# Expert stage of a decoder layer: GpSimd's index copies and carrier arithmetic replaced by ScalarE copies and semaphore increments

## The chip, the core and the metric

The kernel is one program on one core of a Trainium2 chip. The metric is the device time of one execution in microseconds, the median over the runs. TensorE, VectorE (DVE), ScalarE (ACT), GpSimd (POOL) and SyncE (SP) each run their own instruction stream and meet at semaphores. "PE" is TensorE and "DMA" stands for the 16 engines that move data between HBM and the core's memory.

## What is computed

One layer of a decoder: a mixing sub-layer, which the change does not touch, then a layer of 16384 single-neuron experts over 1024 tokens of width 1024. In the reference, cut to what matters:

```python
def peer(h, w_query, sub_keys, expert_u, expert_v):
    ...
    idx = jnp.take_along_axis(cand_i, best_pos, axis=-1)   # 8 heads x 16 experts for each token
    gates = jax.nn.softmax(best_s, axis=-1)
    ...
        u = jnp.take(expert_u, idx_blk, axis=0)
        act = jax.nn.gelu(jnp.einsum('thkd,td->thk', u, h_blk))
        vv = jnp.take(expert_v, idx_blk, axis=0)
        return jnp.einsum('thk,thkd->td', g_blk * act, vv)
```

So each token takes 128 experts; for each of them a row of `expert_u` (1024 floats, 4 KB) is dotted with the token, the result goes through gelu and a gate, and a row of `expert_v` is added with that weight.

## The kernel before, in words

The first 1.43 ms hold the mixing sub-layer, the search for the experts and the making of a dense table of gates. Then comes `experts` (line 1764), in which the change lies, and a short `finish` (line 2188).

`experts` splits the 1024 tokens in two. The first 640 (`DENSE`) are done densely: every expert is computed for every token on TensorE, and a table of gates, mostly zeros, picks what counts. The last 384 tokens, three tiles of 128 (`GATHERED`), fetch their own rows. Both kinds of work are cut into the same 64 steps (`NSTEP`), and a step has 256 experts of the dense kind and, for each of the three gathered tiles, two of the 128 experts that each of its tokens takes, so six row numbers for each partition.

A step c of the dense kind is, in four engines' queues:
- SP loads `un`, rows of expert_u (1 MB; half of it in every fourth step, where an earlier stage has done the other half ahead and only its result `ex_pre` is loaded), `vn`, rows of expert_v (1 MB) and the gate block `w` (640 KB).
- TensorE turns `un` (`turn`, line 1944), multiplies it with the tokens (`hide`, line 1952, 24 matmuls of 320 columns a unit) and multiplies the weighed result with `v` (`share`, line 1959, 10 units of 6 matmuls of 512 columns). In TensorE's step j it hides step j+1, then shares step j with the turns of step j+2 between the shares. Steps have 4 units of hide and turn, but every fourth (`units`) has 2.
- ScalarE splits values into a high part (`h_hi`, `ex_v_hi`, `ex_c_hi`) and does the gelus.
- VectorE makes the low parts (`split_u` line 2093, `split_v` line 2098, line 2137), multiplies by the gates (line 2132) and adds six of the ten share units from PSUM into `acc` (line 2150). `split_v(c+1)` comes once all shares of step c are done; then `weigh` of step c+2, then the adds of step c+1. TensorE has four PSUM banks for what it hands over, and reuses one when the work on it is done (`freed`).

The gathered kind lies between these on VectorE: in each step six dot products of a gathered `u` row with the token (`row_dot`, line 2103, a 128x1024 multiply with reduction) and six multiply-adds of a gathered `v` row (`row_add`, line 2116). Three are in `weigh`, three in `add`. There are three buffers for u rows and three for v rows, so each buffer is used twice a step. VectorE's instruction increments `row_used` when it has done with a buffer.

GpSimd does nothing in this stage but refill those buffers, twelve times a step in a fixed order (`rows`, line 1911). Each `refill` waits for its count of `row_used`, then does a tiny multiply of one column (`carry_wait`, line 1897: the wait is on that instruction, and the gather behind it in the queue has none), and then issues the gather (line 1893), an indirect DMA of 128 rows of 4 KB (512 KB) whose row numbers stand in a tile `ex_row`. For the first refill of a step, `indices` (line 1901) first copies the step's 12 row numbers from `g_row` into one of two `ex_row` tiles at a fixed address, and a `drain` of GpSimd stands between that copy and the gather:

```python
            def refill(c, s, slot, all_rows, to, col, done, n=2 * ROWS):
                pool.wait_ge(row_used, c * SLOTS + slot)
                carry_wait(slot - 1)
                if slot == 1:
                    indices(c, s, n)
                gather(all_rows, to[col % 3], s, col, done[col % 3])
```

Of the kernel before, what the change touches and what calls it, by code (L numbers as in the profile page):

```python
# [22 lines left out]
U32 = mybir.dt.uint32  # L23
ALU = mybir.AluOpType
ACT = mybir.ActivationFunctionType
AX = mybir.AxisListType

P = 128
# [18 lines left out]
GATHERED = 3  # L47
# [1716 lines left out]
def experts(nc, core, t, expert_u, expert_v, h, h_rows, acc, g_row, g_gate, ahead):  # L1764
# [11 lines left out]
    PERIOD = 4  # L1776
    PER = 4 * PERIOD - 2
    ROWS = 2 * GATHERED
    SLOTS = 2 * ROWS
# [7 lines left out]
    u_row = [core.at(f"ex_u_row{k}", 140 + 4 * k, [P, D]) for k in range(3)]  # L1787
    v_row = [core.at(f"ex_v_row{k}", 152 + 4 * k, [P, D]) for k in range(3)]
    row = [core.at(f"ex_row{s}", 94 + s / 16, [P, 2 * ROWS], U32) for s in range(3)]
    dot, act_dot, coef = (core.at(f"ex_{n}", 94.25 + k / 16, [P, ROWS]) for k, n in enumerate(("dot", "act_dot", "coef")))  # L1790
    carry = core.at("ex_carry", 94.5, [P, SLOTS])
    u_rows = expert_u[0].rearrange("(i j) d -> j i d", j=NKEYS)
    v_rows = expert_v[0].rearrange("(i j) d -> j i d", j=NKEYS)
    gates = g_gate[:].rearrange("p n g -> p (n g)")
# [1 line left out]
    u_row_in, v_row_in = core.sems("ex_u_row_in", 3), core.sems("ex_v_row_in", 3)  # L1796
    turned, u_hi, u_lo, v_hi, v_lo, hidden, gelued, weighed, c_hi, c_lo, summed, added = (
        core.sem(f"ex_{n}") for n in ("turned", "u_hi", "u_lo", "v_hi", "v_lo", "hidden", "gelued", "weighed", "c_hi", "c_lo",
                                      "summed", "added"))
    row_used, dotted, dot_gelued, pre_in, cleared = (  # L1800
        core.sem(f"ex_{n}") for n in ("row_used", "dotted", "dot_gelued", "pre_in", "cleared"))

    def units(j):

        return 2 if j % PERIOD == PERIOD - 1 else 4

    def before(i, j, n):


        return i * PER + (j // PERIOD * PER + 4 * (j % PERIOD) + n)  # L1810
# [6 lines left out]
    def ut(hh, e, k, n=1):  # L1817
        at = slice(DENSE + e * P, DENSE + (e + 1) * P)
        return hh[:, k, at] if n == 1 else hh[:, k:k + n, at]
# [20 lines left out]
    NI = NSTEP // PERIOD - 1  # L1840
# [21 lines left out]
    with nc.Block() as block:  # L1862

        @block.sync
        def _(sp):
            load_w(sp, 0, 0)
            load_u(sp, 0, 0)
            load_w(sp, 1, 1)
            load_u(sp, 0, 1)
            load_v(sp, 0)  # L1870
            for half in range(2):
                sp.wait_ge(ahead.stored[half], ahead.BLOCKS * 16)

            def step(i, j, c):
                load_w(sp, c + 2, j % 2)
                load_u(sp, i, j + 2)
                if j == 1:
                    load_pre(sp, i)
                load_v(sp, c + 1)

            with sp.Fori(0, NI) as i:
                for j in range(PERIOD):
                    step(i, j, i * PERIOD + j)
            for j in range(PERIOD - 2):
                step(NI, j, NI * PERIOD + j)
            load_v(sp, NSTEP - 1)

        @block.gpsimd
        def _(pool):
            u_all, v_all = expert_u[0], expert_v[0]  # L1890

            def gather(all_rows, to, s, col, done):
                nc.gpsimd.indirect_dma_start(to[:], None, all_rows, bass.IndirectOffsetOnAxis(row[s][:, col:col + 1], 0)).then_inc(done, 16)  # L1893

            def carry_wait(n):

                nc.gpsimd.tensor_tensor(carry[:, n:n + 1], g_gate[:, 0, 0:1], g_gate[:, 0, 0:1], ALU.mult)  # L1897

            def indices(c, s, n):

                nc.gpsimd.tensor_copy(row[s][:, 0:n], g_rows[:, bass.ds(c * ROWS, n)])
                pool.drain()

            def refill(c, s, slot, all_rows, to, col, done, n=2 * ROWS):

                pool.wait_ge(row_used, c * SLOTS + slot)
                carry_wait(slot - 1)
                if slot == 1:
                    indices(c, s, n)
                gather(all_rows, to[col % 3], s, col, done[col % 3])  # L1910

            def rows(c, s, last=False):
                for k in range(3):
                    refill(c, s, 2 * k + 1, u_all, u_row, 3 + k, u_row_in, ROWS if last else 2 * ROWS)
                    refill(c, s, 2 * k + 2, v_all, v_row, k, v_row_in)
                for k in range(3):
                    if not last:
                        refill(c, s, 2 * k + 7, u_all, u_row, ROWS + k, u_row_in)
                    refill(c, s, 2 * k + 8, v_all, v_row, 3 + k, v_row_in)

            g_rows = g_row[:].rearrange("p n g -> p (n g)")
            nc.gpsimd.tensor_copy(row[2][:, 0:ROWS], g_rows[:, 0:ROWS])
            pool.drain()
            for k in range(3):
                gather(u_all, u_row[k], 2, k, u_row_in[k])
            with pool.Fori(0, NSTEP // 2 - 1) as i:
                for s in range(2):
                    rows(i * 2 + s, s)
            rows(NSTEP - 2, 0)
            rows(NSTEP - 1, 1, last=True)  # L1930

        @block.tensor
# [88 lines left out]
        @block.scalar  # L2021
        def _(act):
            act.sem_inc(u_hi, PRIME)
            act.sem_inc(v_hi, PRIME)
            act.sem_inc(gelued, PRIME)
            act.sem_inc(c_hi, PRIME)

            def split_u(i, j, banks):
                for q in range(units(j)):
                    act.wait_ge(turned, before(i, j, q + 1 + PRIME))  # L2030
                    nc.scalar.activation(ut(h.hi, q // 2, (q % 2) * 4, 4), core.bank[banks[q]].rearrange("p (k n) -> p k n", k=4),  # L2031
                                         ACT.Copy).then_inc(u_hi, 1)

            def split_v(c):
                act.wait_ge(vn_in, c * 16 + 16)
                act.wait_ge(summed, c * NU + PRIME)
                nc.scalar.activation(vh.hi[:], vn[:], ACT.Copy).then_inc(v_hi, 1)  # L2037

            def gelu(i, j, banks):
                c, s = i * PERIOD + j, j % 2  # L2040
                for n in range(4):
                    e, half = n // 2, n % 2
                    x = act_out[n % 2][:] if n < units(j) else pre[:, half, :]
                    if n < units(j):
                        act.wait_ge(hidden, before(i, j, n + 1 + PRIME))
                        act.wait_ge(c_lo, c * 4 + (n - 1 + PRIME))
                        nc.scalar.activation(x, core.bank[banks[n]][:, 0:HD], ACT.Gelu_apprx_tanh).then_inc(gelued, 1)
                    act.wait_ge(weighed, c * 4 + (n + 1 + PRIME))
                    if n == 0:
                        act.wait_ge(summed, c * NU + (PRIME - NU))  # L2050
                    nc.scalar.activation(ch[s].hi[:, e, half * HD:(half + 1) * HD], x, ACT.Copy).then_inc(c_hi, 1)  # L2051

            def gelu_dots(c, part):
                act.wait_ge(dotted, c * 2 + (part + 1))
                to = slice(3 * part, 3 * part + 3)
                nc.scalar.activation(act_dot[:, to], dot[:, to], ACT.Gelu_apprx_tanh).then_inc(dot_gelued, 1)

            def step(i, j, turning=True):
                c = i * PERIOD + j
                gelu_dots(c, 0)  # L2060
                if turning:
                    split_u(i, j + 2, TURN_BANKS[j])
                if j < PERIOD - 1 or turning:
                    split_v(c + 1)
                gelu_dots(c, 1)
                if turning:
                    gelu(i, j + 2, HIDE_BANKS[(j + 1) % PERIOD])

            split_u(0, 0, range(4))
            gelu(0, 0, range(4))  # L2070
            split_u(0, 1, range(4))
            split_v(0)
            gelu(0, 1, HIDE_BANKS[0])
            with act.Fori(0, NI) as i:
                for j in range(PERIOD):
                    step(i, j)
            for j in range(PERIOD):
                step(NI, j, j < PERIOD - 2)

        @block.vector  # L2080
        def _(dve):
# [188 lines left out]
def decoder_layer(nc, x, c, w_mod, b_mod, norm1_g, w_in, b_forget, ln_v_g, w_spatial, b_spatial, w_branch_a, w_branch_b,  # L2270
          w_out, norm2_g, w_query, sub_keys, expert_u, expert_v, final_g, out):
    with ExitStack() as ctx:
        core = Core(nc, ctx)
# [47 lines left out]
        ahead.place("sc", 184, 192)  # L2321
        t.WB = 64
        t.w_dram = core.dram("w_dram", [NKEYS // 2, P, DENSE // t.WB, 2 * t.WB])
        g_row, g_gate = core.at("g_row", 200, [P, P, GATHERED], U32), core.at("g_gate", 201.5, [P, P, GATHERED])
        scatter(nc, core, t, pick_i, pick_j, gate, g_row, g_gate, ahead)
        core.end_second()
        acc = core.at("acc", 0, [P, TT, D])
        experts(nc, core, t, expert_u, expert_v, h2, h_rows, acc, g_row, g_gate, ahead)
        finish(nc, core, t, final_g, acc, out)

# [20 lines left out]
```

## Time and profile before

| | |
|---|---|
| median of 3 runs | 3462.18 us (3461.8 to 3464.92) |
| the profiled execution: its time, its span | 3472.52 us, 3470.8 us |
| `experts`, from the first gather to the last row add | 1432 to 3431 us of the span |
| busy over the span: PE, DVE, ACT, POOL | 3104.2 us (89%), 2614.3 us (75%), 1083.0 us (31%), 1471.4 us (42%) |
| granted TensorE clock, mean of the span | 0.953 |
| DMA moved | 760.68 MB, mean 219 GB/s |

How to read it: the busy share is an average over stages; `experts` is 58% of the span, and there all of TensorE, VectorE and the DMA engines are busy most of the time, so what counts is who waits for whom in a step. A timeline row gives start, duration, engine, line, operation, and in brackets how long the engine was idle before it and what ended the idle time; "issue" is time in which the engine waited for nothing that the profile shows.

### The profile page before, as it was taken

To read this page: it belongs to the slowest core of one execution; us is meant where nothing else is said; L and a number is where in the kernel's file an instruction comes from. 1 tells how busy PE (TensorE), PEld (TensorE's weight loads), DVE (VectorE), ACT (ScalarE), POOL (GpSimd) and SP (SyncE) were. 2 spreads that over 40 slices of the span, in tenths; PEclk is the share of its full clock that TensorE was granted. 3 is DMA by queue.
4 is the path that set the end of the run, shared out by engine and by line. 5 is a ranking of instruction groups with operands and counts; after the bars stand their busy time and mean duration, and the time that the engine had idled before them with its cause. 6 is when DMAs were issued, how large, how long until landed. Compare 5 with 4: busy or idle time off the path is not lost. (4 is left out here: it accounts for less than half of the span.)

```text
span 3470.8 us, 53965 instructions
## 1 busy us (share of the span) xinstructions
PE 3104.2 (89%) x18277; PEld 2734.5 (79%) x18277; DVE 2614.3 (75%) x5246; ACT 1083.0 (31%) x1837; POOL 1471.4 (42%) x1715
## 2 busy tenths in 40 slices
PE   7999999998967788899999999989999999999992
PEld 4998888787756678788788888878887888788881
DVE  5464343553899999488888888888888888888887
ACT  3223666223343366322222222222222222222221
POOL 0001000010355100066666666666666666666664
PEclk9999999998988899999999999999999999999996
DMA  6344432333000168688777887778877778777776
GB/s 245 126 152 147 121 107 77 113 127 113 25 25 0 47 203 268 226 289 304 283 283 297 304 296 293 283 278 302 294 297 286 283 291 311 285 288 293 283 285 236
DMA packets 331852, 760.68 MB, mean 219 GB/s; under 512 B 20348, under 2 KB 171480, under 8 KB 331744
## 3 DMA queue, kind: packets, MB, share of 16 engines
q0 software_dynamic: 115712, 419.48, 32.8%
q1 hardware_dynamic: 214976, 335.65, 28.3%
q10 hardware_dynamic: 1056, 4.19, 0.3%
q8 instruction: 57, 0.93, 0.1%
q14 instruction: 51, 0.42, 0.0%
HBM read 686.86 MB, written 72.39 MB: 219 GB/s over the span
## 5 line engine op out<-in xcount | busy, mean ns | idle before, releaser
L1893 POOL DMA_INDIRECT ex_u_row<-in_expert_u,ex_row x384 | 439.3, 1144 | 450.7 <-issue 431.7
L2116 DVE SCALAR_TENSOR_TENSOR acc<-ex_v_row,ex_coef,acc 128x1024 f32<-128x1024 f32 x384 | 492.4, 1283 | 108.2 <-DMA ex_v_row<-in_expert_v,ex_row 83.7
L1959 PE MATMUL psum<-ex_v_hi,ex_c_lo 128*128 128x512 f32 x1280 | 440.7, 426 | 129.8 <-issue 51.4
L2103 DVE CUSTOM_DVE_ANT_0 ex_u_row<-ex_u_row,h_rows 128x1024 f32<-128x1024 f32 x384 | 469.0, 1221 | 106.9 <-DMA ex_u_row<-in_expert_u,ex_row 106.2
L1893 POOL DMA_INDIRECT ex_v_row<-in_expert_v,ex_row x384 | 458.6, 1194 | 57.0 <-issue 32.4
L1897 POOL TENSOR_TENSOR ex_carry<-g_gate 128x1 f32<-128x1 f32 x765 | 359.1, 469 | 217.9 <-DVE ex_dot L2103 108.8
L1959 PE MATMUL psum<-ex_v_lo,ex_c_hi 128*128 128x512 f32 x1280 | 413.3, 405 | 0.0
L1959 PE MATMUL psum<-ex_v_hi,ex_c_hi 128*128 128x512 f32 x1280 | 408.9, 402 | 0.0
L1959 PEld LDWEIGHTS psum<-ex_v_hi,ex_c_lo 128*128 128x128 f32 x1280 | 226.7, 197 | 177.7 <-issue 102.9
L1952 PE MATMUL psum<-h_hi,h_lo 128*128 128x320 f32 x1792 | 303.6, 312 | 6.9 <-DVE h_lo L2093 4.5
L1952 PE MATMUL psum<-h_lo,h_hi 128*128 128x320 f32 x1792 | 300.6, 310 | 0.0
L1952 PE MATMUL psum<-h_hi 128*128 128x320 f32 x1792 | 299.2, 309 | 0.0
L1959 PEld LDWEIGHTS psum<-ex_v_lo,ex_c_hi 128*128 128x128 f32 x1280 | 250.4, 196 | 59.2
L1959 PEld LDWEIGHTS psum<-ex_v_hi,ex_c_hi 128*128 128x128 f32 x1280 | 249.1, 195 | 58.6
L1952 PEld LDWEIGHTS psum<-h_hi,h_lo 128*128 128x128 f32 x1792 | 274.7, 189 | 19.5 <-issue 11.9
L2150 DVE TENSOR_TENSOR acc<-psum,acc 128x512 f32<-128x512 f32 x384 | 263.3, 686 | 17.0 <-issue 13.1
L1952 PEld LDWEIGHTS psum<-h_lo,h_hi 128*128 128x128 f32 x1792 | 273.7, 189 | 0.0
L1952 PEld LDWEIGHTS psum<-h_hi 128*128 128x128 f32 x1792 | 272.0, 188 | 0.0
L2051 ACT ACTIVATE ex_c_hi<-ex_g 128x320 fp32r<-128x320 f32 x224 | 105.8, 472 | 505.4 <-DVE ex_g L2132 505.4
L2031 ACT ACTIVATE h_hi<-psum 128x512 fp32r<-128x512 f32 x224 | 130.9, 593 | 325.6 <-PE psum L1944 229.3
L2037 ACT ACTIVATE ex_v_hi<-ex_vn 128x2048 fp32r<-128x2048 f32 x64 | 122.8, 1919 | 339.3 <-PE psum L1959 299.9
L2098 DVE TENSOR_TENSOR ex_v_lo<-ex_vn,ex_v_hi 128x2048 fp32r<-128x2048 f32 x64 | 148.8, 2324 | 10.9 <-issue 9.8
(303 smaller groups left out, 5444.6 us busy)
## 6 DMA issues: line engine op xcount, KB each, us to landing
ex_vn<-in_expert_v SPq DMA_DIRECT2D x64, 1024.0 KB
ex_un<-in_expert_u SPq DMA_DIRECT2D x48, 1024.0 KB
w_dram<-sc_w SPq DMA_DIRECT2D x10, 4096.0 KB, 13.5
ex_w<-w_dram SPq DMA_DIRECT2D x64, 640.0 KB
gm_wm<-in_w_mod SPq DMA_DIRECT2D x16, 1024.0 KB, 5.1
pj_raw<-in_w_in SPq DMA_DIRECT2D x11, 1024.0 KB, 7.7
qk_dram<-pj_staged_r POOLq DMA_DIRECT2D x32, 256.0 KB, 3.2
gt_raw<-in_w_in SPq DMA_DIRECT2D x16, 512.0 KB, 3.9
```

The source lines that it names most:

```text
L1893: nc.gpsimd.indirect_dma_start(to[:], None, all_rows, bass.IndirectOffsetOnAxis(row[s][:, col:col + 1], 0)).then_inc(done, 16)
L1897: nc.gpsimd.tensor_tensor(carry[:, n:n + 1], g_gate[:, 0, 0:1], g_gate[:, 0, 0:1], ALU.mult)
L1952: last = nc.tensor.matmul(core.bank[bank][:, 0:HD], lhsT, rhs, start=m == 0, stop=m == len(ops) - 1)
L1959: last = nc.tensor.matmul(out, lhsT, rhs, start=m == 0 and not kept, stop=m == len(ops) - 1, skip_group_check=kept)
L2031: nc.scalar.activation(ut(h.hi, q // 2, (q % 2) * 4, 4), core.bank[banks[q]].rearrange("p (k n) -> p k n", k=4), ACT.Copy).then_inc(u_hi, 1)
L2037: nc.scalar.activation(vh.hi[:], vn[:], ACT.Copy).then_inc(v_hi, 1)
L2051: nc.scalar.activation(ch[s].hi[:, e, half * HD:(half + 1) * HD], x, ACT.Copy).then_inc(c_hi, 1)
L2098: nc.vector.tensor_tensor(vh.lo[:], vn[:], vh.hi[:].bitcast(F32), ALU.subtract).then_inc(v_lo, 1)
L2103: nc.vector.tensor_tensor_reduce(out=u_row[k % 3][:], in0=u_row[k % 3][:], in1=h_rows[:, k % 3, :], scale=1.0, scalar=0.0, op0=ALU.mult, o ...
L2116: nc.vector.scalar_tensor_tensor(out=to, in0=v_row[k % 3][:], scalar=coef[:, k:k + 1], in1=to, op0=ALU.mult, op1=ALU.add).then_inc(row_use ...
L2150: nc.vector.tensor_tensor(to, core.bank[SHARE_BANKS[j][n] if turning else LAST_SHARE_BANKS[j][n]], to, ALU.add).then_inc(added, 1)
```

## The change

The tiny multiply before each gather becomes an increment of a semaphore that nobody waits on (`carried`), issued by GpSimd behind the same wait. The copy of the row numbers and the drain leave GpSimd. ScalarE makes that copy in each step for the step after, behind its second small gelu (`gelu_dots(c, 1)`), and GpSimd's first refill of a step waits for ScalarE's count (`indexed`). `g_row` is kept as float32, as ScalarE reads it, and the copy converts to uint32. Step 0's numbers are copied before the stage's first split.

```diff
-    carry = core.at("ex_carry", 94.5, [P, SLOTS])
...
-            def carry_wait(n):
-
-                nc.gpsimd.tensor_tensor(carry[:, n:n + 1], g_gate[:, 0, 0:1], g_gate[:, 0, 0:1], ALU.mult)
-
-            def indices(c, s, n):
-
-                nc.gpsimd.tensor_copy(row[s][:, 0:n], g_rows[:, bass.ds(c * ROWS, n)])
-                pool.drain()
-
-            def refill(c, s, slot, all_rows, to, col, done, n=2 * ROWS):
+            def refill(c, s, slot, all_rows, to, col, done):
 
                 pool.wait_ge(row_used, c * SLOTS + slot)
-                carry_wait(slot - 1)
                 if slot == 1:
-                    indices(c, s, n)
+                    pool.wait_ge(indexed, c + 2)
+                pool.sem_inc(carried, 1)
                 gather(all_rows, to[col % 3], s, col, done[col % 3])
...
-            g_rows = g_row[:].rearrange("p n g -> p (n g)")
-            nc.gpsimd.tensor_copy(row[2][:, 0:ROWS], g_rows[:, 0:ROWS])
-            pool.drain()
+            pool.wait_ge(indexed, 1)
+            pool.sem_inc(carried, 1)
...
+            def indices(c, s, n=2 * ROWS):
+
+                nc.scalar.activation(row[s][:, 0:n], g_rows[:, bass.ds(c * ROWS, n)], ACT.Copy).then_inc(indexed, 1)
+
+            def step(i, j, turning=True, final=False):
                 c = i * PERIOD + j
                 gelu_dots(c, 0)
...
                 gelu_dots(c, 1)
+                if not final:
+                    indices(c + 1, (j + 1) % 2, 2 * ROWS if turning or j < PERIOD - 2 else ROWS)
                 if turning:
                     gelu(i, j + 2, HIDE_BANKS[(j + 1) % PERIOD])
 
+            indices(0, 2)
+            indices(0, 0)
...
-        g_row, g_gate = core.at("g_row", 200, [P, P, GATHERED], U32), core.at("g_gate", 201.5, [P, P, GATHERED])
+        g_row, g_gate = core.at("g_row", 200, [P, P, GATHERED]), core.at("g_gate", 201.5, [P, P, GATHERED])
```

## Rows read from the trace of the kernel before

**Rows 1.** Busy by stretch, expert stage: us, PE, PEld, DVE, ACT, POOL, clock, DMA share, GB/s

```profile
1480.00:3400.00 1920.00, 1790.02 (x9828) 1583.65 (x9826) 1634.02 (x2405) 461.35 (x871) 1244.66 (x1565) 0.97 0.79 291
```

**Rows 2.** Waits of VectorE, 1480 to 3440: waiter, releaser, us in total, times, longest

```profile
DVE ex_u_row L2103 <- DMA ex_u_row<-in_expert_u,ex_row: 106.2, 85, 3.5
DVE acc L2116 <- DMA ex_v_row<-in_expert_v,ex_row: 83.7, 55, 3.8
```

**Rows 3.** Timeline of GpSimd: the stage's first step, then a step in its middle

```profile
1471.99 0.19 POOL L1901 COPY ex_row<-g_row 128x12 uint32 x1
1473.23 1.00 POOL L1893 DMA_INDIRECT ex_u_row<-in_expert_u,ex_row  x1 [1.05 <-issue]
...
2422.61 0.45 POOL L1901 COPY ex_row<-g_row 128x12 uint32 x1
2429.34 1.53 POOL L1893 DMA_INDIRECT ex_u_row<-in_expert_u,ex_row  x1 [6.28 <-issue]
...
2432.68 0.98 POOL L1893 DMA_INDIRECT ex_u_row<-in_expert_u,ex_row  x1 [0.15 <-issue]
```

**Rows 4.** Waits of GpSimd, 1500 to 3420

```profile
POOL ex_u_row L1893 <- issue: 429.0, 248, 8.5
```

**Rows 5.** By source line, whole span: duration ns min/median/max, first and last start

```profile
L1897 POOL TENSOR_TENSOR ex_carry<-g_gate x765: 194/212/1647, 1471.7 to 3425.9; 128x1 f32<-128x1 f32 x192
L1893 POOL DMA_INDIRECT ex_u_row<-in_expert_u,ex_row x384: 944/978/3037, 1431.9 to 3415.6; - x192
```

**Rows 6.** Busy by short stretches, columns as in rows 1

```profile
2427.00:2430.00 3.00, 3.00 (x20) 2.65 (x19) 2.79 (x5) 0.44 (x1) 0.66 (x1) 1.00 0.06 26
2444.00:2448.00 4.00, 3.90 (x26) 3.45 (x24) 3.79 (x6) 2.13 (x2) 2.21 (x5) 1.00 1.03 421
```

**Rows 7.** Timeline of TensorE: the first hide matmuls of eight of its steps

```profile
1495.38 1.33 PE L1952 MATMUL psum<-h_hi,h_lo 128*128 128x320 f32 x8
...
1524.06 1.33 PE L1952 MATMUL psum<-h_hi,h_lo 128*128 128x320 f32 x8
...
2444.83 1.43 PE L1952 MATMUL psum<-h_hi,h_lo 128*128 128x320 f32 x8
...
2474.61 1.33 PE L1952 MATMUL psum<-h_hi,h_lo 128*128 128x320 f32 x8
...
2503.30 1.35 PE L1952 MATMUL psum<-h_hi,h_lo 128*128 128x320 f32 x8
...
2536.83 1.33 PE L1952 MATMUL psum<-h_hi,h_lo 128*128 128x320 f32 x8
...
2567.67 1.44 PE L1952 MATMUL psum<-h_hi,h_lo 128*128 128x320 f32 x8
...
3336.62 1.41 PE L1952 MATMUL psum<-h_hi,h_lo 128*128 128x320 f32 x8
```

**Rows 8.** Timeline of VectorE: three v splits, one first add, one dot

```profile
1498.33 2.29 DVE L2098 TENSOR_TENSOR ex_v_lo<-ex_vn,ex_v_hi 128x2048 fp32r<-128x2048 f32 x1 [0.17 <-issue]
...
1528.10 2.29 DVE L2098 TENSOR_TENSOR ex_v_lo<-ex_vn,ex_v_hi 128x2048 fp32r<-128x2048 f32 x1 [0.17 <-issue]
...
1541.77 0.68 DVE L2150 TENSOR_TENSOR acc<-psum,acc 128x512 f32<-128x512 f32 x1
...
2434.26 1.23 DVE L2103 CUSTOM_DVE_ANT_0 ex_u_row<-ex_u_row,h_rows 128x1024 f32<-128x1024 f32 x1 [1.61 <-DMA ex_u_row<-in_expert_u,ex_row]
...
2511.84 2.29 DVE L2098 TENSOR_TENSOR ex_v_lo<-ex_vn,ex_v_hi 128x2048 fp32r<-128x2048 f32 x1 [0.16 <-issue]
```

**Rows 9.** Timeline of TensorE: the end of its long wait in the step of 2503

```profile
2526.24 1.22 PE L1959 MATMUL psum<-ex_v_hi,ex_c_lo 128*128 128x512 f32 x2 [3.60 <-issue]
```

**Rows 10.** By source line, ScalarE's small gelu of the dots: duration ns min/median/max

```profile
L2056 ACT ACTIVATE ex_act_dot<-ex_dot x128: 183/188/209, 1481.3 to 3423.9; 128x3 f32<-128x3 f32 x128
```

**Rows 11.** Waits of VectorE in the stage's tail, 3368 to 3435

```profile
DVE ex_u_row L2103 <- DMA ex_u_row<-in_expert_u,ex_row: 8.0, 3, 3.5
DVE acc L2116 <- DMA ex_v_row<-in_expert_v,ex_row: 4.2, 4, 1.3
```

More of the change, by code:

```diff
@@ L1799, in experts @@
                                       "summed", "added"))
-    row_used, dotted, dot_gelued, pre_in, cleared = (
-        core.sem(f"ex_{n}") for n in ("row_used", "dotted", "dot_gelued", "pre_in", "cleared"))
+    row_used, dotted, dot_gelued, pre_in, cleared, indexed, carried = (
+        core.sem(f"ex_{n}") for n in ("row_used", "dotted", "dot_gelued", "pre_in", "cleared", "indexed", "carried"))
+    g_rows = g_row[:].rearrange("p n g -> p (n g)")
     def units(j):
@@ L1913, in rows @@
                 for k in range(3):
-                    refill(c, s, 2 * k + 1, u_all, u_row, 3 + k, u_row_in, ROWS if last else 2 * ROWS)
+                    refill(c, s, 2 * k + 1, u_all, u_row, 3 + k, u_row_in)
                     refill(c, s, 2 * k + 2, v_all, v_row, k, v_row_in)
@@ L2056, in gelu_dots @@
                 nc.scalar.activation(act_dot[:, to], dot[:, to], ACT.Gelu_apprx_tanh).then_inc(dot_gelued, 1)
-            def step(i, j, turning=True):
+            def indices(c, s, n=2 * ROWS):
+                nc.scalar.activation(row[s][:, 0:n], g_rows[:, bass.ds(c * ROWS, n)], ACT.Copy).then_inc(indexed, 1)
+            def step(i, j, turning=True, final=False):
                 c = i * PERIOD + j
@@ L2077, in _ @@
             for j in range(PERIOD):
-                step(NI, j, j < PERIOD - 2)
+                step(NI, j, j < PERIOD - 2, j == PERIOD - 1)
         @block.vector
```

## The prediction

> **What bounds the kernel now.** I first read the busy time of the expert stage by stretches [rows 1]: of 1920 us TensorE is busy 93%, VectorE 85%, the DMA engines 79% at 291 GB/s, GpSimd 65%, ScalarE 24%. No engine is full, so the next view is who waits. VectorE waits 106.2 us for gathered u rows and 83.7 us for gathered v rows [rows 2], though each buffer has half a step between two uses. So the gathers are issued late, and the timeline of GpSimd says why [rows 3]: behind the copy of the row numbers the next gather starts 6.28 us later, with GpSimd waiting for nothing that the profile shows. Only the drain stands between the two. In the stage's first step, where the only gathers so far had been issued 40 us before [rows 5], the same gap is 1.05 us. Such gaps add up to 429.0 us, the longest 8.5 [rows 4]; other gathers have 0.15 us before them [rows 3], so with 248 - 64 = 184 of those at 0.15, 401 us lie behind the 64 copies, 6.3 us each. While it lasts the DMA engines run empty: share 0.06 and 26 GB/s from 2427 to 2430, against 421 GB/s from 2444 to 2448 [rows 6]. I read this as a drain that holds GpSimd until its gathers in flight have landed. The cost reaches VectorE as a late row (the dot at 2434.26 waited for one [rows 8]), and TensorE through VectorE.
>
> How much reaches the end is read from TensorE's steps [rows 7]. Sixty steps, fifteen periods of four, run from 1495.38 to 3336.62: 122.75 us a period, 30.69 a step. One period, begun at 2444.83, has steps of 29.78 (A), 28.69 (B), 33.53 (C) and 30.84 us (D). C is the step with 2 units of hide instead of 4, so it ought to be TensorE's shortest; in it TensorE waits for VectorE, at last 3.60 us [rows 9]. Call S the start of TensorE's hides and T the start of VectorE's split_v. In C T-S was 2511.84 - 2503.30 = 8.54 us; in a step where VectorE is on time it is 1498.33 - 1495.38 = 2.95 [rows 7, 8]. From T to the end of the first add, which gives TensorE its bank back, is 1541.77 + 0.68 - 1528.10 = 14.35 us of VectorE's own work [rows 8]. In the step of 2503 this gives 2511.84 + 14.35 = 2526.19, and TensorE resumes at 2526.24 [rows 9]. From there to the next S are 10.6 us (2536.83 - 2526.2). So C = (T-S) + 14.35 + 10.6: TensorE's short step is set by VectorE.
>
> **The change part by part.**
> *The drain goes.* Rows then never have to make up 6.3 us of lost issuing. A gather takes 2434.26 - 2429.34 = 4.9 us from issue to use with the queue empty [rows 3, 8]. Twelve row operations on six buffers bring a buffer round every 14.6 us, so some 13 us are left for it. I take VectorE's waits inside the periods as gone. Then T-S in C falls to 2.95 and C becomes 2.95 + 14.35 + 10.6 = 27.9; another C, begun at 1524.06, has T-S of 4.04, which shows that the term varies with lateness, and I take 28.1. D has the units of A and should fall to A's 29.78; I take 29.9 for some time at the lower clock after C's wait. A and B already run at TensorE's pace and stay. Sum: 29.78 + 28.69 + 28.1 + 29.9 = 116.5 us, 6.3 less than 122.75; times 15 is 94 us.
> *The tail.* The last steps have few or no hides, so VectorE sets the end, and it waits 8.0 + 4.2 us for rows [rows 11]. The last rows depend on the last dots, so I count 9 of these 12.
> *The carriers.* 765 multiplies of 0.21 us median, up to 1.65, leave GpSimd [rows 5] and increments come in. GpSimd is not the bound once the drain is gone: 1244.66 us busy in 62.6 steps is 19.9 us of a 29 us step. Counted at nothing; the cover is those 9 us of GpSimd. If the increment cost nothing the gathers start up to 0.4 us earlier, which only adds to the 13 us. No row shows an increment on GpSimd in this stage; below, nothing; above, what the drain costs (a rival).
> *The copy on ScalarE.* 65 instructions of about 0.19 us, the price of a small activation [rows 10]. They stand behind the second small gelu and ahead of the gelus of the hides. ScalarE is busy 24% [rows 1]. Counted at nothing. Without cover it would cost 65 x 0.19 = 12 us.
> *The new wait.* GpSimd's first refill of step c+1 waits for a copy that ScalarE makes right after its split of v, while the refill needs the first dot of the next weigh, behind VectorE's 2.29 us split of v [rows 8]. The copy is there about 3 us before. Queued behind the wait are only gathers.
> *DMA.* The same bytes: 291 GB/s x 30.69 us = 8.9 MB a step, at 29.1 us a step 307 GB/s, below the 421 seen. SP's loads are not moved. Without the drain they share the engines with gathers at all times.
> The DMA page of the Trainium skill ("DMA: Bandwidth & Descriptors", Specifications) gives about 358 GB/s as HBM's limit for a core. The row of 421 GB/s over 4 us speaks against that as a ceiling here; with it the mean demand would still fit, and only in VectorE's weigh (six gathers and vn, 4.2 MB in 11.5 us) would some 0.2 us a step be missing, an estimate of 13 us less gain.
>
> **Sum.** 94 + 9 = 103 us. The profiled execution took 3472.5, so 3369.5; it stands 10.3 us above the median of the runs shown, so the median is forecast at 3359 us.
>
> **Rivals.**
> *Rows stay late in part.* The gathers, now always queued, and SP's loads press on each other, or a gather under load takes over 13 us. For: the engines are full (share 1.03) in bursts [rows 6]. Against: a mean share of 0.79 x 30.69 / 29.1 = 0.83. If half of the 190 us of waits stay, half of the gain stays: 3462 - 52 = 3410 us. The same page (Queues, rings and completion order) says that each DMA engine takes the queue rows in turn, packet by packet, which would halve SP's rate beside a full gather queue; no number here hangs on it.
> *A larger gain.* If the wait in C also becomes too short for the clock to fall behind it, and VectorE itself runs freer without GpSimd's arithmetic: the mean clock of 0.97 [rows 1] is worth 3% of 122.75 = 3.7 us a period, of which I put 1.5 behind this wait (its first two matmuls take 1.22 us [rows 9]), so 15 x 1.5 us, and up to 15 us more: 3359 - 38 = 3321 us.
> The SBUF page of the Trainium skill ("SBUF — State Buffer", Summary) says that a VectorE instruction with two SBUF inputs and a GpSimd one that reads SBUF block each other, the second waiting the first out. The 1647 ns carriers agree; for VectorE it would mean up to five carriers of 0.2 us in each C, 15 us, which no row shows.
> *No change.* The gap is not the drain but something each step's first gather pays. For: it is always at that gather. Against: 1.05 us in the first step. Time: 3460 us.
> *Slower.* A semaphore increment on GpSimd waits, as the drain does, for the gathers in flight. Place: before each of the twelve gathers of a step. It decides from the point where one gather with its increment takes over 29.1 / 12 = 2.4 us. With the 6.3 us of the drain and 0.98 of the gather it is 7.3 x 12 = 87 us a step, so 87 - 30.7 = 56 us more a step, and the kernel would take 3462 + 64 x 56 = 7050 us. Against: the increment is not meant to order anything; for: only that no row shows one.
>
> **How the numbers follow.** Forecast 73%, rows late in part 14%, larger gain 5%, no change 4%, slower 4%. Range: the forecast's own unknowns are C at 27.9 to 28.6 and D at 29.8 to 30.8 (+-15 us), ScalarE's 12 us and the tail's 9; it reaches down to most of the larger gain, 3325, and up to the partial case, 3415. A measurement of this kernel can tell 0.2%, 7 us, from no change. Faster by more than that 92%, within 4%, slower 4%.
>
> **What would show it.** Right: no gap over 2 us between gathers where VectorE had freed the buffer; VectorE's waits for rows under 30 us in total; T-S in C about 3 us; C about 28 and a period about 116.5; no stretch of 3 us with DMA under 0.1. TensorE still waits some 4 us in each C for the first add. Wrong in size: T-S in C stays above 4, or A and B lengthen (loads of SP late, seen as ScalarE's split of v or TensorE's turns waiting). Wrong in kind: gaps of 5 us before each step's first gather, or before every gather.

## The result, and the profile after

The changed kernel takes 3365.06 us (median of 4 runs, 3361.81 to 3366.06), beside 3463.55 us for the kernel before on the same chip: a ratio of 0.9713, 95% interval 0.9697 to 0.973, or 98.5 us less. Forecast were 3359 us in a range of 3325 to 3415. The saving in us differs between chips, through the kernel before: on another chip that takes 3452.27 us and the changed kernel 3364.79 (e6 below), so 87.5 us less.

Busy time by stretch over the expert stage, with the columns of [rows 1] (us, PE, PEld, DVE, ACT, POOL, clock, DMA share, GB/s):

```profile
1480.00:3300.00 1820.00, 1755.78 (x9833) 1573.24 (x9833) 1646.14 (x2412) 472.37 (x931) 975.76 (x752) 0.98 0.87 308
```

TensorE is now busy 96% of the stage (93% before), VectorE 90% (85%), and the DMA engines move 308 GB/s instead of 291. Then the waits of GpSimd from 1480 to 3340, and those of VectorE, which answer to [rows 4] and [rows 2]:

```profile
POOL ex_u_row L1893 <- DVE ex_dot L2101: 421.3, 240, 3.4
POOL ex_v_row L1893 <- DVE acc L2114: 327.5, 189, 3.2
POOL ex_v_row L1893 <- issue: 58.5, 192, 0.3
POOL ex_u_row L1893 <- issue: 44.3, 138, 2.5
```

```profile
DVE acc L2114 <- DMA ex_v_row<-in_expert_v,ex_row: 3.6, 2, 2.9
```

GpSimd now stands idle because VectorE has not yet freed a buffer, which is how it should be; the unexplained gaps of up to 8.5 us are gone (the longest is 2.5 us, once, at the stage's end). VectorE's waits for rows fell from 189.9 us to under 4. The timeline of GpSimd around a step's first gather, to hold against [rows 3]:

```profile
2423.62 0.94 POOL L1893 DMA_INDIRECT ex_u_row<-in_expert_u,ex_row  x1 [1.17 <-DVE ex_dot L2101]
2425.72 2.46 POOL L1893 DMA_INDIRECT ex_v_row<-in_expert_v,ex_row  x1 [1.16 <-DVE acc L2114]
2429.79 1.76 POOL L1893 DMA_INDIRECT ex_u_row<-in_expert_u,ex_row  x1 [1.62 <-DVE ex_dot L2101]
2431.86 1.24 POOL L1893 DMA_INDIRECT ex_v_row<-in_expert_v,ex_row  x1 [0.30 <-issue]
```

The gather at 2429.79 is the first of its step: 1.62 us before it instead of 6.28, and they are a wait for the dot that frees its buffer. The increments show as 0.30 us ahead of a gather that waits for nothing else.

The steps of TensorE (first hide matmuls) and VectorE (split of v, first add of C), which answer to [rows 7, 8, 9]; S and T are as in the prediction:

```profile
1492.66 1.33 PE L1942 MATMUL psum<-h_hi,h_lo 128*128 128x320 f32 x8
...
1521.35 1.33 PE L1942 MATMUL psum<-h_hi,h_lo 128*128 128x320 f32 x8
...
1538.64 0.72 PE L1949 MATMUL psum<-ex_v_hi,ex_c_lo 128*128 128x512 f32 x2 [3.65 <-DVE acc L2148]
...
1549.51 1.33 PE L1942 MATMUL psum<-h_hi,h_lo 128*128 128x320 f32 x8
...
1579.18 1.33 PE L1942 MATMUL psum<-h_hi,h_lo 128*128 128x320 f32 x8
...
1608.87 1.33 PE L1942 MATMUL psum<-h_hi,h_lo 128*128 128x320 f32 x8
...
3234.91 1.33 PE L1942 MATMUL psum<-h_hi,h_lo 128*128 128x320 f32 x8
```

```profile
1524.29 2.29 DVE L2096 TENSOR_TENSOR ex_v_lo<-ex_vn,ex_v_hi 128x2048 fp32r<-128x2048 f32 x1 [0.16 <-issue]
...
1537.90 0.68 DVE L2148 TENSOR_TENSOR acc<-psum,acc 128x512 f32<-128x512 f32 x1
```

B takes 28.69 us, C 28.16, D 29.67, A 29.69, and every later period repeats this within 0.2 us, while before the same steps scattered by several: the fifteen C lay between 29.29 and 33.53 us, with a mean of 32.48, and the means of A, B and D were 30.37, 28.82 and 31.07. T-S in C is 1524.29 - 1521.35 = 2.94, T to the end of the first add 14.29, and what is left of C is one wait of TensorE of 3.65 us. Sixty steps now take 3234.91 - 1492.66 = 1742.25 us, or 116.15 a period, against 1841.24 before.

### The profile page after: what moved, and what is told of

The parts are those of the page before. It is cut to its first block and busy times, and to the rows that moved or that the text cites. A ratio compares the mean times of both kernels' runs of the same rounds, so it can differ in the third digit from the quotient of the medians.

```text
span 3360.1 us, 53961 instructions
## 1 busy us (share of the span) xinstructions
PE 3065.8 (91%) x18277; PEld 2718.8 (81%) x18277; DVE 2617.2 (78%) x5246; ACT 1095.9 (33%) x1902; POOL 1195.1 (36%) x885
## 5 line engine op out<-in xcount | busy, mean ns | idle before, releaser
L1893 POOL DMA_INDIRECT ex_u_row<-in_expert_u,ex_row x384 | 475.1, 1237 | 731.4 <-DVE ex_dot L2101 421.3
L1893 POOL DMA_INDIRECT ex_v_row<-in_expert_v,ex_row x384 | 519.3, 1352 | 386.9 <-DVE acc L2114 327.5
L1949 PE MATMUL psum<-ex_v_hi,ex_c_lo 128*128 128x512 f32 x1280 | 427.8, 416 | 64.2 <-DVE acc L2148 54.8
L1949 PE MATMUL psum<-ex_v_lo,ex_c_hi 128*128 128x512 f32 x1280 | 406.2, 399 | 0.0
L2037 ACT ACTIVATE ex_g<-psum 128x320 f32<-128x320 f32 x224 | 98.3, 439 | 315.1 <-PE psum L1942 314.0
L2091 DVE TENSOR_TENSOR h_lo<-psum,h_hi 128x512 fp32r<-128x512 f32 x224 | 153.6, 687 | 43.0 <-ACT h_hi L2021 42.8
```

What stands on the lines that cost most here:

```text
L1949: last = nc.tensor.matmul(out, lhsT, rhs, start=m == 0 and not kept, stop=m == len(ops) - 1, skip_group_check=kept)
L2091: nc.vector.tensor_tensor(ut(h.lo, q // 2, (q % 2) * 4, 4), core.bank[bank].rearrange("p (k n) -> p k n", k=4), ut(h.hi, q // 2, (q % 2) * ...
```

## The experiments

Theory 1 was mine: GpSimd's drain waits until the gathers in flight have landed, and the gain is its removal. Theory 2: arithmetic on GpSimd, beside VectorE and beside the gathers, is what costs, and the multiplies matter most. Theory 3: each step's first gather pays, whatever stands before it. Each run is timed against the kernel before on its own chip; that took 3452.3 us (e1 to e4), 3452.27 us (e5 to e8) and 3447.38 us (e9, e10). Of each edit the lines that matter are shown, with "..." where lines are left out; semaphores' declarations and the like are left out everywhere.

**The copy on GpSimd, with a semaphore in the drain's place (e1)**

```diff
-                nc.gpsimd.tensor_copy(row[s][:, 0:n], g_rows[:, bass.ds(c * ROWS, n)])
-                pool.drain()
+                nc.gpsimd.tensor_copy(row[s][:, 0:n], g_rows[:, bass.ds(c * ROWS, n)]).then_inc(copied, 1)
+                pool.wait_ge(copied, c + 2)
+                pool.sem_inc(carried, 1)
...
```

> The kernel before, with one thing undone: behind GpSimd's copy of the row numbers it waits for that copy's own semaphore increment instead of draining. The copy and the twelve multiplies a step stay on GpSimd. Theory 1 (the drain waits for the gathers in flight, and that alone is the gain): the time of the changed kernel, 3365 us within 10; gap between copy and gather under 1.5 us; T-S in every fourth step 2.9 us. Theory 2 (arithmetic on GpSimd beside VectorE and the gathers is what costs): 3440 us or more. Theory 3 (each step's first gather pays, whatever stands before it): 3463 us, with the gap of 6 us still there.

Measured: 3364.37 us, ratio 0.9747 (0.9731 to 0.9763). T-S in C 2.94, C 28.09. Its GpSimd at a step's first gather (timeline):

```profile
2402.56 0.38 POOL L1897 TENSOR_TENSOR ex_carry<-g_gate 128x1 f32<-128x1 f32 x1 [0.77 <-DVE ex_dot L2105]
2402.88 0.19 POOL L1901 COPY ex_row<-g_row 128x12 uint32 x1
2403.88 1.30 POOL L1893 DMA_INDIRECT ex_u_row<-in_expert_u,ex_row  x1 [0.81 <-POOL ex_row L1901]
```

The same copy, multiply and gather as before, and 0.81 us between copy and gather instead of 6.28. This one exchange gives the whole gain: by its ratio and by its time it is the changed kernel. Theory 3 falls with it, and so does theory 2 as the account of the gain.

**Increments for the multiplies, copy and drain kept (e2)**

```diff
-                nc.gpsimd.tensor_tensor(carry[:, n:n + 1], g_gate[:, 0, 0:1], g_gate[:, 0, 0:1], ALU.mult)
+                pool.sem_inc(carried, 1)
```

> The kernel before with the 765 multiplies replaced by semaphore increments; GpSimd's copy and drain stay. Theory 1: 3463 us within 10, gaps of about 6 us behind the copies. Theory 2: most of the gain, 3365 to 3400 us. If an increment waited for gathers in flight, as a drain does, it would be slower than 4000 us.

Measured: 3427.52 us (3418.71 to 3443.02), ratio 0.9921 (0.9905 to 0.9938). The drain's gaps are there (7.9 us the longest), and so is most of the time; but 25 us (0.8%) are gone, more than theory 1 allows. An increment does not wait for gathers. The executions scatter by 24 us, and the trace is of the slowest.

**The multiplies back, no drain (e3)**

```diff
-                pool.sem_inc(carried, 1)
+                    pool.sem_inc(carried, 1)
+                    pool.wait_ge(ticked, c * SLOTS + 1)
+                    pool.sem_inc(carried, 1)
+                nc.gpsimd.tensor_tensor(carry[:, slot - 1:slot], g_gate[:, 0, 0:1], g_gate[:, 0, 0:1], ALU.mult).then_inc(ticked, 1)
```

> The changed kernel with the multiplies back in the place of the increments (each also counts on a semaphore, on which GpSimd waits a step later, long after it is done); the copy stays on ScalarE and there is no drain. Theory 1: 3365 us within 10, since GpSimd has some 10 us a step to spare. Theory 2: 3400 us or more, and VectorE's work from T to its first add longer than 14.30 us.

Measured: 3363.47 us, ratio 0.9743 (0.9727 to 0.9759); T to the first add 14.31. Its busy time by stretch:

```profile
1480.00:3300.00 1820.00, 1755.69 (x9836) 1573.08 (x9835) 1645.91 (x2412) 473.14 (x934) 1144.47 (x1505) 0.98 0.87 308
```

GpSimd is busy 169 us more than in the changed kernel and nothing else moves: without a drain the multiplies are free.

**The drain put back, no arithmetic on GpSimd (e4)**

```diff
                 pool.sem_inc(carried, 1)
+                if slot == 1:
+                    pool.drain()
                 gather(all_rows, to[col % 3], s, col, done[col % 3])
```

> The changed kernel with one thing added: GpSimd drains before each step's first gather, with no arithmetic on it at all. Theory 1: 3463 us within 15, gap of about 6 us before those gathers, DMA engines empty for 2 to 3 us behind it. Theories 2 and 3: 3365 us.

Measured: 3423.65 us (3407.33 to 3452.05), ratio 0.9903 (0.9876 to 0.9929). The drain alone costs 59 us (3423.65 against some 3364 without it), where theories 2 and 3 had nothing; but theory 1's 3463 within 15 is missed too, by 39 us. The trace is of the slowest execution, 3452.05 us. The gaps ahead of the 63 first gathers have a median of 8.15 us; one of them, and the busy time around it:

```profile
2409.40 2.15 POOL L1893 DMA_INDIRECT ex_v_row<-in_expert_v,ex_row  x1 [0.30 <-issue]
2419.70 1.82 POOL L1893 DMA_INDIRECT ex_u_row<-in_expert_u,ex_row  x1 [8.15 <-DVE ex_dot L2103]
```

```profile
2412.00:2415.00 3.00, 3.00 (x22) 3.00 (x21) 2.93 (x7) 0.49 (x3) 0.00 (x0) 1.00 0.78 266
2415.00:2418.00 3.00, 3.00 (x22) 2.96 (x21) 3.00 (x6) 0.65 (x3) 0.00 (x0) 1.00 0.63 244
2418.00:2421.00 3.00, 3.00 (x17) 2.47 (x16) 2.79 (x5) 0.50 (x2) 1.30 (x1) 1.00 0.05 20
```

The profile puts this gap down to VectorE's dot, which had ended at 2412.3; the other 7.4 us are the drain. The DMA engines run dry before the next gather is issued, with nothing on GpSimd but gathers and increments.

The four kernels make a square. With a drain: 3452 with multiplies, 3426 without (the mean of the two runs). Without: 3363 to 3365 either way. So the two costs are not a sum. VectorE's waits for rows go the same way: 190 us in the kernel before, 141 in e2, 163 in e4, 3 in e1 and in e3. My reading of the traces of how they meet: after a drain GpSimd has a backlog and issues at its own pace, and there each gather follows the last in 1.49 us on average with a multiply between, in 1.36 to 1.38 with an increment (pitches under 1.9 us, 355 to 387 of them). With no backlog the pace is VectorE's. That the pace explains all of the 27 us was not tested by itself.

**Waiting for the landing instead of draining (e5)**

```diff
+                if slot == 1 and landed:
+                    for k in range(3):
+                        pool.wait_ge(u_row_in[k], c * 32 + 16)
+                        pool.sem_inc(carried, 1)
+                        pool.wait_ge(v_row_in[k], c * 32)
+                        pool.sem_inc(carried, 1)
```

> The changed kernel, no drain; instead GpSimd waits before each step's first gather on the six row semaphores until all gathers issued so far have landed. If the drain's cost is exactly a wait for the landing (theory 1), this run is like the one with the drain put back: gaps before the first gathers 5.4 to 9 us (there: median 8.15), DMA engines empty behind it, 3424 us within 20. If the drain waits for less (only for the making of the gathers' descriptors, say), the gaps here are longer by over 1 us and the time is higher; if it waits for more, they are shorter by over 1 us.

Measured: 3395.49 us (3387.1 to 3405.71), ratio 0.9837 (0.9811 to 0.9862). That is faster than the 3424 within 20 of theory 1. The gaps have a median of 6.66 us and a mean of 6.87 (433 us over 63), against 8.15 and 7.97 (502 over 63) with the drain. VectorE waits 71 us for rows. Two of the gaps:

```profile
2353.88 2.15 POOL L1893 DMA_INDIRECT ex_v_row<-in_expert_v,ex_row  x1 [0.30 <-issue]
2362.51 1.58 POOL L1893 DMA_INDIRECT ex_u_row<-in_expert_u,ex_row  x1 [6.48 <-DVE acc L2122]
...
2412.38 2.15 POOL L1893 DMA_INDIRECT ex_v_row<-in_expert_v,ex_row  x1 [0.30 <-issue]
2422.17 1.14 POOL L1893 DMA_INDIRECT ex_u_row<-in_expert_u,ex_row  x1 [7.64 <-DVE ex_dot L2109]
```

So a wait for the landing explains most of the drain's gap but not all, and costs 31 us where the drain costs 59. The gaps of the two traces, 1.1 to 1.5 us apart, do not measure the drain itself, since the gathers in flight also landed at another time. The packets of the gathers do. With the drain, the next gather starts 1.57 us (median; 1.53 to 1.79) after the last of them: at 2419.70 above, after a last packet that ended at 2418.11. By queue, 2415.00 to 2418.13 and then 2418.14 to 2419.70 (packets, MB, share of the 16 engines; the gathers are q0, SP's loads q1):

```profile
q1 hardware_dynamic: 112, 0.41, 32.3%
q0 software_dynamic: 99, 0.34, 29.3%
...
q1 hardware_dynamic: 15, 0.05, 7.8%
```

In the kernel before and in e2 it is 1.56 and 1.57 us. With the wait for the landing it is 1.10 us (1.06 to 1.40): at 2362.51, after 2361.43. So the drain never ends before the landing, and takes 0.47 us more than the wait. The other 1 us is that the last packet itself came later behind the last gather's issue, 6.56 us against 5.58. Over 63 steps 0.47 us is 30 us, near the 28 us between the medians; whether that is all of it was not tested, nor what the drain does in the 0.47 us.

**The changed kernel again (e6).** It stands beside the two that follow.

> The changed kernel once more, to stand beside the two that follow: 3365 us within 10.

Measured: 3364.79 us, ratio 0.9747 (0.9732 to 0.9761).

**What bounds it now: a row add behind C's first add (e7).** The formula for C says that TensorE's wait there is VectorE's order of work. `late` is true for the row work around step C alone.

```diff
...
+                            if n < 2 or not late:
                                 row_add(adds, 3 + n)
...
                         split_u(i, j + 2, n, TURN_BANKS[j][n])
+                    if late and n == 0:
+                        row_add(c - 1, 5)
```

> The changed kernel; in every fourth step (C, where TensorE waits 3.65 us for VectorE's first add) one row add of 1.2 us moves from ahead of that add to behind it and behind the split that follows it. Theory (C is set by T-S + 14.30 + the rest): TensorE's wait falls from 3.65 to 2.45 us, C from 28.1 to 26.9, so 16 x 1.2 = 19 us less, 3346 us; if the clock no longer falls behind the shorter wait, up to 26 us more. Rival (TensorE would then wait for the next bank instead): no change, 3365 us.

Measured: 3336.81 us, ratio 0.9667 (0.9653 to 0.9682), 28 us less than the changed kernel beside it. TensorE's wait in C (timeline):

```profile
1539.57 0.73 PE L1949 MATMUL psum<-ex_v_hi,ex_c_lo 128*128 128x512 f32 x2 [2.46 <-DVE acc L2149]
```

It fell by the 1.2 us moved, and C fell by 1.83, from a mean of 28.10 to one of 26.27. The other 0.6 us are the clock. In the changed kernel TensorE's granted clock falls to 0.50, the lower of its two levels (1.2 GHz), in every C, about when TensorE resumes from its wait, and is back at 1.00 before the step ends. In the C whose wait ends at 1538.64:

```profile
1540.00:1543.00 3.00, 3.00 (x11) 2.42 (x10) 2.93 (x7) 0.60 (x1) 0.94 (x1) 0.50 0.86 285
```

With the row add late it falls in every second C, 7 of 15. Two C that follow each other, one without a fall and one with:

```profile
1523.48:1549.17 25.69, 23.18 (x126) 19.71 (x124) 24.41 (x38) 7.14 (x14) 13.80 (x11) 1.00 0.86 298
1637.22:1664.15 26.93, 24.48 (x126) 21.06 (x124) 25.65 (x40) 7.14 (x14) 13.81 (x11) 0.94 0.86 295
```

The eight C without take 25.67 to 25.71 us and the seven with take 26.91 to 26.95, behind the same wait of 2.45 us. So one fall costs 1.24 us, and eight falls fewer in fifteen are 0.66 us a period.

**A dot as well (e8)**

```diff
...
+                    if late and n == 0:
+                        row_dot(c, 2)
+                        row_add(c - 1, 5)
...
+                if j == 2 and turning:
+                    split_u(i, j + 2, TURN_BANKS[j], 0, 1)
                 gelu_dots(c, 0)
```

> As the run before, with one dot of 1.2 us moved too, behind the same add and split, and ScalarE's small gelu of the dots behind its first split of u in that step. Theory: 2.4 us less wait ahead of the first add, but the second add then comes 2.4 us late against a slack of some 1.6 us; TensorE's wait about 1.3 + 0.8 us: 16 x 1.6 = 26 us less than the changed kernel, 3340 us, and more (to 3315) if the clock stays up. Rival: the second wait takes all back, 3365 us.

Measured: 3337.35 us, ratio 0.9663 (0.9649 to 0.9677), the same as the run before. Waits of TensorE, and the busy time from the start of the first C to 3238:

```profile
PE psum L1949 <- DVE acc L2151: 45.7, 30, 1.6
```

```profile
1526.34:3238.00 1711.66, 1665.94 (x9470) 1492.61 (x9469) 1566.32 (x2309) 453.35 (x900) 945.52 (x719) 1.00 0.89 314
```

Thirty waits instead of fifteen: the first (1.6 us) and now the second add (1.4 us) hold TensorE, 3.05 us a period in all. The granted clock stays at 1.00 in every C, which gives back the seven falls of the run before, 0.58 us a period; the waits, 0.6 us longer in all, take as much. So C is 26.24, as before.

**The row work of C spread, one pair late (e9)**

```diff
...
+                    rows = [(row_dot, c, 3), (row_add, c, 0), (row_dot, c, 4), (row_add, c, 1), (row_dot, c, 5), (row_add, c, 2)]
+                    if late:
+                        rows = [(row_dot, c, 2), (row_add, c - 1, 5)] + rows
+                    for what, of, k in rows[n:] if n == NU - 1 else rows[n:n + 1]:
+                        what(of, k)
```

> As the run with a dot and an add moved behind the first add of C, but the two are spread: in that step each of the six adds is followed by one row operation, all row operations one pair late, and the last three stand behind the sixth add. The first wait of TensorE in C stays 1.6 us, the second (1.4 us, for the second add) should go, since that add comes 1.2 us sooner: C from 26.24 to about 24.9, 15 x 1.3 = 20 us less than 3337, so 3317 us. Rival: VectorE is then late at the start of the next step (T-S in D above 5.5 us, up to where D lengthens) and gives part of it back: 3325 to 3337 us.

Measured: 3315.5 us (3313.41 to 3319.61), ratio 0.9607 (0.9586 to 0.9628). Waits of TensorE and one of the steps, from its S to the next:

```profile
PE psum L1949 <- DVE acc L2151: 24.6, 15, 1.6
```

```profile
1527.34 1.33 PE L1942 MATMUL psum<-h_hi,h_lo 128*128 128x320 f32 x8
1551.89 1.33 PE L1942 MATMUL psum<-h_hi,h_lo 128*128 128x320 f32 x8
1581.86 1.33 PE L1942 MATMUL psum<-h_hi,h_lo 128*128 128x320 f32 x8
```

The second wait is gone, the granted clock stays at 1.00, C is 24.55, and D gives back 0.3 of it (29.97), with T-S there at 6.33. This version beats both kernels: by the ratios to the kernel before, 1.4% or 48 us less than the change.

**The first add itself sooner (e10)**

```diff
...
+                    if late and n == 2:
+                        add_one(c - 1, 0, (SHARE_BANKS if turning else LAST_SHARE_BANKS)[2][0])
```

> As e9, with the first add itself taken ahead of VectorE's last unit of weigh (about 1 us sooner). TensorE's first wait in C falls from 1.6 to 0.6 us, but the turn behind it now waits for the split that stayed where it was, so at most a part of that: 0 to 15 us less than e9, 3302 to 3317 us. Rival: the split's bank is the bound, same time as e9.

Measured: 3317.28 us, ratio 0.9614 (0.9593 to 0.9635): no gain. C falls to 24.05 and D rises to 30.56. Waits of TensorE:

```profile
PE psum L1949 <- DVE acc L2151: 12.3, 30, 0.6
PE psum L1934 <- DVE h_lo L2093: 6.9, 15, 0.5
```

In C the wait for the first add shrinks from 1.64 to 0.2 us, but the turns now wait 0.46 us for the split of u that stayed. T-S in D is 6.93, so VectorE starts 4.0 us late there, and TensorE waits 0.57 us for an add in D, where it waited for none in e9: what C gains, D gives back.

## Why the prediction was right, and where not

*What bounds, right.* The gap was the drain; it emptied the DMA engines, made rows late on VectorE, and reached TensorE in the short step C. e1, e4 and the profile after each show one link of it. That the gap was a wait for the landing is shown by the packets of the gathers (e5). C was not the only door: of the 6.6 us that a period gained, 4.4 came from C, 1.4 from D and 0.7 from A, whose mean before was 30.37 us. "A and B already run at TensorE's pace and stay" was read from one period, which had an A of 29.78; the forecast put 5.4 us on C and 0.9 on D, and its total came out near because it was taken from the mean of all fifteen.

*The sum.* Forecast were A 29.78, B 28.69, C 28.1, D 29.9, in all 116.5 us a period; measured 29.69, 28.69, 28.10, 29.68, in all 116.15. (D had no time at the lower clock: 1.00 in all fifteen.) The fifteen periods gave 1841.24 - 1742.25 = 99.0 us, forecast 94. The tail, from the last S to the end of the span, went from 3470.8 - 3336.62 = 134.2 to 3360.1 - 3234.91 = 125.2: 9.0 us, forecast 9. The profiled execution gained 110.7 us, the remaining 2.7 of which lie ahead of the first S, nearly all (2.3) ahead of the stage's first gather, in work that the change doesn't touch. The medians gained 98.5: the profiled execution of before stood some 9 us above its median and the one after 3 below it, so the 10.3 us that the forecast took off to come from the profiled execution to the median belong to one execution of the kernel before. The sum of the steps, 3369.5, was 8 us above the changed kernel's profiled execution, and with the offset off it the forecast was 6 us below the median: that the two errors partly cancel is luck.

*T-S, right and the key.* T-S in C fell to 2.94 (forecast 2.95), and TensorE still waits 3.65 us there (forecast some 4). No stretch of 3 us in the stage has a DMA share below 0.26, where the forecast asked for none under 0.1.

*The copy on ScalarE, right.* In the trace it takes 0.20 us behind the small gelu of 0.19, with ScalarE then waiting 1.50 us for TensorE:

```profile
1494.68 0.19 ACT L2046 ACTIVATE ex_act_dot<-ex_dot 128x3 f32<-128x3 f32 x1
1494.77 0.20 ACT L2050 ACTIVATE ex_row<-g_row 128x12 uint32 x1
1496.47 0.44 ACT L2037 ACTIVATE ex_g<-psum 128x320 f32<-128x320 f32 x1 [1.50 <-PE psum L1942]
```

Moving it there was not needed, as e1 shows.

*The carriers, right as a term, incomplete as a statement.* "Counted at nothing" holds for the change, since the cover it named (GpSimd's spare time) is there once the drain is gone. The prediction did not see that in the kernel before they cost 25 to 29 us, beside the drain: GpSimd, as I read it, had no spare time in the catching up behind one. The gain of the drain's removal by itself is therefore all of it from the kernel before, but only 59 us from a kernel without multiplies.

*The drain as a wait for the landing, right in kind, short by about 0.5 us* (e5).

*The rivals.* Rows late in part: VectorE waited under 4 us for rows, with the DMA engines at a share of 0.87. So neither the ceiling of 358 GB/s nor the taking of turns with SP's loads, both of which the prediction quotes from the Trainium skill ("DMA: Bandwidth & Descriptors", Specifications and Queues, rings and completion order), showed in the time. No change and slower fell in e4 and e2. A larger gain: the fall of the clock in C is worth 1.24 us a period (e7), where the prediction supposed 1.5, and it is still there in every C of the changed kernel; only less waiting gives it back (e7 to e9). The Trainium skill's rule on VectorE and GpSimd sharing an SBUF interface ("SBUF — State Buffer", Summary) would let the multiplies slow VectorE: T to the first add is 14.31 us with them (e3) and 14.30 without, so next to nothing of it is seen here.

## What to carry to other kernels

On GpSimd, order a gather behind the making of its indices with a semaphore that the making increments, and not with a drain: the drain also waits for the gathers in flight. The same small instructions on an engine off the critical path were free in one kernel (e3) and worth 25 us in another (e2); before calling them either, look whether there is a stretch in which the engine has to catch up. When one engine's steps are uneven (in e9 TensorE is busy for 22.9 us of C, against the 29.7 of A) and its partner's are even, the short step is where the partner's order of work sets the time.

## What the runs showed of the hardware that I had not expected

A drain on GpSimd lasted until its indirect DMAs had landed: the next gather started 1.5 to 1.8 us after their last packet in three traces, where a wait for their semaphores took 1.1 us. That made 6.3 us a time in the kernel before. TensorE's granted clock fell to half behind a wait of 3.65 us every time, behind one of 2.45 us every second time, and behind one of 1.64 us, or two of 1.6 and 1.4 us in one step, not at all; a fall cost 1.24 us. A semaphore increment on GpSimd, also behind a wait, leaves 0.30 us between two gathers, and the gathers can still follow each other in 1.24 us. The kernels with a drain scatter (3407 to 3452 us for one, in four executions), those without stay within some 6 us. That each wait, since it depends on when rows land, sets up the next would explain it, but no run tests that.
